# Scores of chunk 0 one projection sooner, copied from PSUM into the tile they are searched in, and its experts chosen in one go

## The chip, the cores and the metric

The kernel runs on one NeuronCore of one Trainium2 chip. The time is that of the whole kernel on the device, in microseconds (us). TensorE is PE, VectorE is DVE, ScalarE is ACT, GpSimd is POOL and SyncE is SP; each takes its instructions in the order in which they are written, and waits on semaphores.

## What is computed

One layer of a decoder trunk on 1024 tokens of 1024 channels. A mixer of four branches ends in an output projection and a layer norm. Then each token picks 16 experts for each of 8 heads out of 16384 (a product of two lists of 128 keys), and adds their value rows, weighted.

```
def peer_ffn(x, w_q, sub_k1, sub_k2, u_tab, v_tab):
    q = (xt @ w_q).reshape(T, PEER_HEADS, 2, PEER_DQ // 2)
    s1 = jnp.einsum('thc,nc->thn', q[:, :, 0], sub_k1, preferred_element_type=jnp.float32)
    s2 = jnp.einsum('thc,nc->thn', q[:, :, 1], sub_k2, preferred_element_type=jnp.float32)
    v1, i1 = lax.top_k(s1, PEER_TOPK)
    v2, i2 = lax.top_k(s2, PEER_TOPK)
    ...
    top_s, top_j = lax.top_k(cand_s, PEER_TOPK)
    idx = jnp.take_along_axis(cand_i, top_j, axis=-1)
    g = jax.nn.softmax(top_s, axis=-1).astype(x.dtype)
    ...
        act = jax.nn.gelu(jnp.einsum('cd,ced->ce', xb, u_tab[ib]), approximate=False)
        return jnp.einsum('ce,ced->cd', gb * act, v_tab[ib])
```

`x = layer_norm(ALPHA * x + mix)` stands ahead of it, and `x = layer_norm(ALPHA * x + ffn)` behind it.

## The kernel before

The 1024 tokens are eight chunks of 128. The first 1305 us are the mixer's branches, which the change leaves alone. The function `ffn` does the rest. It has one program per engine, and the order of all work in it is written out by hand.

First PE folds the query weights and the keys into one matrix (`fold`), so that scores are x times that matrix. Then comes the stage that the change touches, which I call the projections. It has 16 steps, in the order of the list `SEQ`. A step ("m", c) is chunk c's output projection (`mixed`, 48 matmuls at line 1196) and its layer norm on DVE (`first_norm`, lines 1459 to 1462 and 1433 to 1450). A step ("x", c) is chunk c's scores (`scored`, 4 quarters of 48 matmuls, lines 65 to 67), which ACT copies out of PSUM, 512 columns at a time, at line 1322. I write m0, x0 and so on.

Each step needs its input turned round. PE transposes it (`turn`, line 1172, 8 transposes), ACT writes its high half (`high`, line 1296), DVE its low half (`low`, line 1454). There are two buffers, so the turn of a step is issued one step ahead: in step i PE does `turn(i + 1)` and then the matmuls of step i. `turn(i + 1)` waits until `low(i)` is done (semaphore `t_lo`), and where step i + 1 is an x step it also waits for that chunk's layer norm (`normed`). On DVE step i is `low(i + 1)`, then `first_norm` of an m step, then whatever else is hung on that step.

What is hung there is the choice of experts (`choose`, 136 pieces numbered k: lines 1476 to 1587) and the first gathered rows (`row`, line 1652). For even chunks (0, 2, 4, 6) rows of the tables u and v are gathered by POOL (line 1147) into a ring of five buffers at first, and multiplied on DVE; 128 rows of u and 128 of v per chunk. Odd chunks go through PE instead (table blocks, lines 1239 and 1282). POOL starts when `chosen` says that chunk 0's experts are known.

The scores of every chunk go from PSUM to the tile `score_out` (`stage`), from there to HBM, and from there to the tile `scores_in` (`sco`), in which `choose` searches and which it overwrites. Chunk 0's choice is in two parts: pieces 0 to 69 in the step of x1, pieces 70 to 135 in the step of x2. The exponentials of a choice are made by ACT (`exps`, line 1300), at fixed places of ACT's program: chunk 0's after the copies of x2, chunk 1's after table block 2. Chunk 1's choice is spread over rows 3 to 40 (`CHOICE_AT`); its last pieces, from k = 133 on, stand ahead of row 40 and wait for those exponentials. `D_ROWS` says how many rows are done in which step: 8 rows in each of the steps x3 to x7. The rows behind them follow when all scores are done.

The first lines of PE's loop, which sets the order:

```
        for i, (kind, c) in enumerate(SEQ):
            if i + 1 < len(SEQ):
                turn(i + 1)
            (mixed if kind == "m" else scored)(i, c)
```

Of the kernel before, what the change touches and what calls it, by code (L numbers as in the profile page):

```python
# [7 lines left out]
ACT = mybir.ActivationFunctionType  # L8
# [10 lines left out]
NCH = T // P  # L19
# [19 lines left out]
RWS = 1.0 / WS  # L39
# [681 lines left out]
def merge(nc, ctx, M, A):  # L721
# [91 lines left out]
    def _(dve):  # L813
# [21 lines left out]
                        nc.vector.tensor_tensor(out, out, tmp[c % 2][:], ALU.add)  # L835


SEQ = [("m", 0), ("m", 1), ("m", 2), ("x", 0), ("m", 3), ("x", 1), ("m", 4), ("x", 2), ("m", 5), ("x", 3),
       ("m", 6), ("x", 4), ("m", 7), ("x", 5), ("x", 6), ("x", 7)]
M_STEP = {c: i for i, (kind, c) in enumerate(SEQ) if kind == "m"}  # L840
X_STEP = {c: i for i, (kind, c) in enumerate(SEQ) if kind == "x"}
GS = 4096.0
# [3 lines left out]
NT = 136  # L846
# [114 lines left out]
for _w, _n in enumerate((128, 128 + 46, 128 + 78, 256)):  # L961
    for _q in range(32):
        ONEHOT_AT.setdefault(_n + _q, []).append((_w, _q))
D_ROWS = {X_STEP[3]: (0, 8), X_STEP[4]: (8, 16), X_STEP[5]: (16, 24), X_STEP[6]: (24, 32), X_STEP[7]: (32, 40)}


def ffn(nc, ctx, M, A, out):
    sem = lambda n: ctx.enter_context(nc.semaphore(n))
    Tt, ps, ident = M["T"], M["ps"], M["ident"]
    big, hl, ln, stage, sco = (M[n] for n in "big hl ln stage sco".split())  # L970
# [38 lines left out]
    s_mm, s_out, s_stored, x1_stored = (sem(n) for n in "s_mm s_out s_stored x1_stored".split())  # L1009
    sc_in, sc_free, exp_in, exp_out = (sem(n) for n in "sc_in sc_free exp_in exp_out".split())  # L1010
# [22 lines left out]
    @block.sync  # L1033
    def _(sp):
        for b in range(2):
            sp.dma_start(wqt[b], A["w_qt"][b]).then_inc(wq_in[b], 16)
        sp.dma_start(kt[:, 0, :], A["k1_t"]).then_inc(keys_in, 16)
        sp.dma_start(kt[:, 1, :], A["k2_t"]).then_inc(keys_in, 16)
        for i in range(2):
            sp.dma_start(xin[i], A["x"][P * i:P * i + P]).then_inc(x_in[i], 16)  # L1040
        sp.dma_start(ln[:], A["ln"][:, 0:2]).then_inc(ln_in, 16)
        sp.dma_start(iota[:], A["iota"]).then_inc(ln_in, 16)
        for b in range(2, 2 * H):
            sp.wait_ge(fold_mm, 2 * b - 2)
            sp.dma_start(wqt[b % 2], A["w_qt"][b]).then_inc(wq_in[b % 2], 16)
            if b < KD:
                sp.wait_ge(wo_ready, b - 1)
                sp.dma_start(wof[b % 2], A["w_o"][b]).then_inc(wo_in[b % 2], 16)
        for i, (kind, c) in enumerate(SEQ):
            if kind == "m":  # L1050
                if c + 2 < NCH:
                    sp.wait_ge(summed, c + 1)
                    sp.dma_start(xin[c % 2], A["x"][P * (c + 2):P * (c + 3)]).then_inc(x_in[c % 2], 16)
                if c % 2:
                    sp.wait_ge(normed, c + 1)
                    sp.dma_start(A["x1"][c // 2], x1[c]).then_inc(x1_stored, 16)
            else:
                sp.wait_ge(s_out, 4 * c + 4)
                sp.dma_start(A["scores"][c], stage[:]).then_inc(s_stored, 16)
                if c == 0:  # L1060
                    sp.wait_ge(s_stored, 16)
                    sp.dma_start(sco[:], A["scores"][0]).then_inc(sc_in, 16)
                elif c == 2:
                    sp.wait_ge(sc_free, 1)
                    sp.dma_start(sco[:], A["scores"][1]).then_inc(sc_in, 16)
        sp.wait_ge(x1_stored, 16 * ND)
        sp.wait_ge(s_stored, 16 * NCH)
        def choice_load(k):
            sp.wait_ge(sc_free, k)
            sp.dma_start(sco[:], A["scores"][CHOICES[k]]).then_inc(sc_in, 16)  # L1070

        def weights_store(w):
            sp.wait_ge(w_out, 32 * w + 32)
            for a in range(4):
                sp.dma_start(A["weights"][32 * a:32 * a + 32, :, P * w:P * w + P].rearrange("b e t -> e b t"),
                             wst[:, 32 * a:32 * a + 32, :]).then_inc(w_st, 16)

        choice_load(2)
        choice_load(3)
        choice_load(4)  # L1080
        weights_store(0)
        choice_load(5)
        weights_store(1)
        weights_store(2)
        choice_load(6)
        weights_store(3)

        def weights_load(j):
            if j < NEXP // P:
                sp.dma_start(pr[j % NPR], A["weights"][BLOCK[j]]).then_inc(w_in[j // 4 % (NPR // 4)], 16)  # L1090

        def value_load(h, i):
            if h < 2 * NG:
                s, hf = divmod(h, 2)
                sp.dma_start(vt[i], A["v_blocks"][BLOCK[GB * s + i], :, DT * hf:DT * hf + DT]).then_inc(v_in[i // 2], 16)

        sp.wait_ge(w_st, 64 * ND)
        for j in range(4):
            weights_load(j)
            b = BLOCK[j]  # L1100
            sp.wait_ge(h_st[b % 4], 16 * (b // 4 + 1))
            sp.dma_start(ht[j], A["h"][b]).then_inc(h_first, 16)
            value_load(0, j)
        for j in range(4, GB):
            weights_load(j)
            value_load(0, j)
        for j in range(GB, NPR):
            weights_load(j)
        for i in range(4):
            sp.wait_ge(h_st[i], 16 * (NPRE // 4))  # L1110
        sp.dma_start(ln[:], A["ln"][:, 2:4]).then_inc(ln_in, 16)
        for h in range(2 * NG):
            s, hf = divmod(h, 2)
            for i in range(GB):
                sp.wait_ge(v_mm, GB * h + i + 1)
                value_load(h + 1, i)
                if hf:
                    weights_load(GB * s + i + NPR)
            if h == 26:
                sp.wait_ge(sc_free, NCH)  # L1120
                for d in range(2):
                    sp.dma_start(again[d], A["x1"][d]).then_inc(again_in, 16)
        for d in range(ND):
            sp.wait_ge(dense_done, d + 1)
            c = 2 * d + 1
            sp.dma_start(out[P * c:P * c + P, :], dense[d]).then_inc(stored, 16)
            if d < 2:
                sp.dma_start(again[d], A["x1"][d + 2]).then_inc(again_in, 16)
        sp.wait_ge(stored, 16 * ND)
        sp.wait_ge(sparse_stored, 16 * ND)  # L1130
        sp.wait_ge(again_in, 16 * ND)
# [32 lines left out]
    def _(pe):  # L1164
        def turn(i):
            kind, c = SEQ[i]
            if i:
                pe.wait_ge(t_lo, i)
            if kind == "x":
                pe.wait_ge(normed, c + 1)  # L1170
            for k in range(KD):
                m = pe.transpose(ps[:, k // 4, P * (k % 4):P * (k % 4) + P], x1[c][:, P * k:P * k + P], ident[:])
            m.then_inc(turned, 1)
# [44 lines left out]
        pe.wait_ge(fold_lo, 4 * KD)  # L1218
# [3 lines that stand above are left out]
# [68 lines left out]
    def _(act):  # L1290
# [7 lines left out]
        def exps(k):  # L1298
            act.wait_ge(exp_in, k + 1)
            act.activation(gx[:], gx[:], ACT.Exp).then_inc(exp_out, 1)  # L1300
# [13 lines left out]
        for i, (kind, c) in enumerate(SEQ):  # L1314
            if i + 1 < len(SEQ):
                high(i + 1)
            if kind == "x":
                for q in range(4):
                    act.wait_ge(s_mm, 4 * c + q + 1)
                    if c and q == 0:  # L1320
                        act.wait_ge(s_stored, 16 * c)
                    act.activation(stage[:, 512 * q:512 * q + 512], ps[:, 6 + q % 2, :], ACT.Copy, scale=RWS
                                   ).then_inc(s_out, 1)
            if i == X_STEP[2]:
                exps(0)
        for i in range(NUT):
            act.dma_start(ut[i], A["u_t"][i]).then_inc(u_in[i], 16)
# [98 lines left out]
    def _(dve):  # L1426
# [40 lines left out]
        def choose(c, k):  # L1467

            o = CHOICES.index(c)
            if k == 0:  # L1470
                if o == 7:
                    dve.wait_ge(sc_late, 16)
                else:
                    dve.wait_ge(sc_in, 16 * o + 16)
            if k < 16:
                nc.vector.max(v16[:, k, 0:8], sc[:, k, :])
                if k == 15:
# [206 lines left out]
        for i, (kind, c) in enumerate(SEQ):  # L1684
            if i + 1 < len(SEQ):
                low(i + 1)
            if kind == "m":
                first_norm(c)
            if i == X_STEP[1]:
                for k in range(0, 70):  # L1690
                    choose(0, k)
            if i == X_STEP[2]:
                for k in range(70, NT):
                    choose(0, k)
            for n in range(*D_ROWS.get(i, (0, 0))):
                row(n)
        dve.wait_ge(s_mm, 4 * NCH)
        for n in range(D_ROWS[X_STEP[7]][1], NROW):
            row(n)
# [196 lines left out]
```

## Time and profile before

| | us |
|---|---|
| median of three runs | 4133.27 (4126.22 to 4134.67) |
| the profiled execution | 4116.23 |
| its span in the trace | 4114.4 |
| PE, DVE, ACT, POOL busy | 3472.6, 2654.8, 997.8, 1468.6 |
| the projections (first matmul to last copy of scores) | about 1370 to 1642 |
| table blocks and gathered rows behind them | 1642 to the end |

The profiled execution is 17 us (0.4%) below the median of the runs. Times in the trace are counted from the span's start. In the projections PE is busy without a break but for one; behind them PE, DVE and the DMA engines share the work, and none of them is busy all the time.

### The profile page before, as it was taken

To read this page: it belongs to the slowest core of one execution; us is meant where nothing else is said; L and a number is where in the kernel's file an instruction comes from. 1 tells how busy PE (TensorE), PEld (TensorE's weight loads), DVE (VectorE), ACT (ScalarE), POOL (GpSimd) and SP (SyncE) were. 2 spreads that over 40 slices of the span, in tenths; PEclk is the share of its full clock that TensorE was granted. 3 is DMA by queue.
4 is the path that set the end of the run, shared out by engine and by line. 5 is a ranking of instruction groups with operands and counts; after the bars stand their busy time and mean duration, and the time that the engine had idled before them with its cause. 6 is when DMAs were issued, how large, how long until landed. Compare 5 with 4: busy or idle time off the path is not lost.

```text
span 4114.4 us, 43940 instructions
## 1 busy us (share of the span) xinstructions
PE 3472.6 (84%) x15340; PEld 1928.6 (47%) x15340; DVE 2654.8 (65%) x5144; ACT 997.8 (24%) x2241; POOL 1468.6 (36%) x1155
## 2 busy tenths in 40 slices
PE   8988998899998899993778876969867598888685
PEld 3445675688887544441334342424323243333232
DVE  1993463233223488698975973887788667777777
ACT  3324232322222211115496380000000000000000
POOL 2220000012110012354343243656655656566652
PEclk9998697799999999996889988989989799899887
DMA  3110000111102235887968979989988999999995
GB/s 104 51 41 6 1 1 1 72 47 47 63 32 88 94 118 189 289 323 236 306 223 275 315 251 362 375 289 354 364 311 304 330 370 351 331 351 350 340 344 188
DMA packets 323966, 873.03 MB, mean 212 GB/s; under 512 B 30120, under 2 KB 96168, under 8 KB 319024
## 3 DMA queue, kind: packets, MB, share of 16 engines
q0 software_dynamic: 154256, 560.01, 37.8%
q1 hardware_dynamic: 139552, 222.25, 15.6%
q10 hardware_dynamic: 29952, 88.09, 6.0%
q8 instruction: 121, 1.98, 0.2%
q14 instruction: 85, 0.70, 0.1%
HBM read 801.03 MB, written 69.21 MB: 212 GB/s over the span
## 4 chain that ended last, share of the span: by engine, by line
DMA 24%; DVE 16%; PE 10%; ACT 7%; issue 4%; POOL 4%; SPq 1%; DVEq 1%; ACTq 0%
DMA tiles<-v,expert_ids 10%; DMA tiles<-u,expert_ids 7%; DVE tiles L1652 4%; PE ps L1239 4%; POOL tiles L1147 3%; DVE row_t_pairs L1658 3%; ACT score_out L1355 3%; DMA ring_extra<-u,expert_ids 2%; ACT tiles L1354 2%; PE ps L1196 2%; DMA shared_64k<-h_kept 2%; DVE tiles L1625 1%; PE ps L65 1%; PE ps L66 1%; PE ps L67 1%
## 5 line engine op out<-in xcount | busy, mean ns | idle before, releaser
L1282 PE MATMUL ps<-shared_64k 128*128 128x512 f32 x2048 | 943.9, 624 | 300.3 <-ACT score_out L1416 265.7
L1239 PE MATMUL ps<-tiles 128*128 128x512 f32 x2048 | 925.4, 611 | 3.3 <-DMA tiles<-u_t 3.3
L1147 POOL DMA_INDIRECT tiles<-u,expert_ids x437 | 536.1, 1227 | 751.8 <-DVE hidden_sums L1652 371.3
L1282 PEld LDWEIGHTS ps<-shared_64k 128*128 128x128 f32 x2048 | 408.1, 201 | 835.0 <-issue 549.3
L1147 POOL DMA_INDIRECT tiles<-v,expert_ids x438 | 534.8, 1221 | 520.3 <-DVE row_t_pairs L1658 383.5
L1658 DVE SCALAR_TENSOR_TENSOR row_t_pairs<-tiles,hidden_sums,row_t_pairs 128x1024 f32<-128x1024 f32 x432 | 550.4, 1281 | 186.9 <-DMA tiles<-v,expert_ids 184.0
L1239 PEld LDWEIGHTS ps<-tiles 128*128 128x128 f32 x2048 | 399.7, 197 | 497.4 <-issue 497.4
L1652 DVE CUSTOM_DVE_ANT_0 tiles<-tiles 128x1024 f32<-128x1024 f32 x437 | 530.8, 1220 | 151.8 <-DMA tiles<-u,expert_ids 147.3
L785 POOL TENSOR_TENSOR strip_lo<-strip_f,strip_hi 128x3072 f16<-128x3072 f32 x15 | 90.2, 6014 | 825.5 <-ACT strip_f L758 825.5
L65 PE MATMUL ps<-strip_hi,x_hi_t 128*128 128x256 f16 x1024 | 279.9, 273 | 15.2 <-DVE strip_lo L818 10.5
L66 PE MATMUL ps<-strip_lo,x_hi_t 128*128 128x256 f16 x1024 | 279.9, 273 | 0.0
L67 PE MATMUL ps<-strip_hi,x_lo_t 128*128 128x256 f16 x1024 | 279.9, 273 | 0.0
L1416 ACT ACTIVATE score_out<-ps 128x512 f32<-128x512 f32 x128 | 66.0, 602 | 871.1 <-DVE tiles L1625 681.3
L1257 PE MATMUL ps<-tiles 128*128 128x128 f16 x512 | 72.9, 232 | 181.3 <-ACT score_out L1355 100.1
L1354 ACT ACTIVATE tiles<-score_out,picks_t 128x128 f16<-128x128 f16 x512 | 202.8, 396 | 31.0 <-DVE score_out L1601 31.0
L1355 ACT ACTIVATE score_out<-score_out,picks_t 128x128 f16<-128x128 f16 x512 | 202.4, 395 | 0.0
L832 DVE SCALAR_TENSOR_TENSOR product<-ps,gate 128x256 f32<-128x256 f32 x96 | 40.6, 423 | 238.0 <-PE ps L67 177.1
L306 DVE SCALAR_TENSOR_TENSOR conv_acc<-conv_in,dw_sb,conv_acc x120 | 175.5, 1538 | 0.0
L65 PE MATMUL ps<-x_hi_t,w_hi 128*128 128x512 f16 x400 | 152.4, 381 | 13.2 <-DVE x_lo_t L285 13.2
L199 POOL TENSOR_TENSOR w_lo<-w_f,w_hi 128x1024 f16<-128x1024 f32 x28 | 70.4, 2513 | 255.7 <-ACT w_f L116 255.7
L66 PE MATMUL ps<-x_lo_t,w_hi 128*128 128x512 f16 x400 | 152.2, 380 | 0.0
L67 PE MATMUL ps<-x_hi_t,w_lo 128*128 128x512 f16 x400 | 152.1, 380 | 0.0
(263 smaller groups left out, 5234.0 us busy)
## 6 DMA issues: line engine op xcount, KB each, us to landing
tiles<-u_t ACTq DMA_DIRECT2D x128, 512.0 KB, 6.8
shared_64k<-v SPq DMA_DIRECT2D x256, 256.0 KB, 6.4
weights_kept<-shared_64k SPq DMA_DIRECT2D x16, 2048.0 KB, 25.8
shared_64k<-weights_kept SPq DMA_DIRECT2D x128, 256.0 KB, 8.7
strip_f<-strips SPq DMA_DIRECT2D x15, 1536.0 KB, 6.3
h_kept<-ln_sb ACTq DMA_DIRECT2D x80, 256.0 KB, 5.8
shared_64k<-h_kept POOLq DMA_DIRECT2D x76, 256.0 KB, 6.5
w_f<-w_t SPq DMA_DIRECT2D x30, 512.0 KB, 3.6
```

Source lines behind the costliest of these rows:

```text
L65: pe.matmul(out, a_hi, b_hi, start=first, stop=False)
L66: pe.matmul(out, a_hi, b_lo, start=False, stop=False)
L67: return pe.matmul(out, a_lo, b_hi, start=False, stop=last)
L306: nc.vector.scalar_tensor_tensor(acc, src, w, acc, ALU.mult, ALU.add).then_inc(tap, 1)
L785: nc.gpsimd.tensor_tensor(sl[s][:], sf[s][:], sh[s][:], ALU.subtract).then_inc(ready, 1)
L1147: nc.gpsimd.indirect_dma_start(ring[R_SLOT[n]], None, A["u" if r < NSEL else "v"], bass.IndirectOffsetOnAxis(ap=idx[:, g, e:e + 1], axis=0 ...
L1239: m = pe.matmul(ps[:, bank, :], ut[u % NUT][:, k, :], x1t[:, k, :], start=k == 0, stop=k == KD - 1)
L1282: m = pe.matmul(ps[:, 4 + t, :], pr[j % NPR][:, P * t:P * t + P], vt[i], start=i == 0, stop=i == GB - 1)
L1354: act.activation(ah[:, n % 4, t, :], o1[:, n % 4, t, :], ACT.Copy, scale=pt[:, 3, tok])
L1355: ins = act.activation(o1[:, n % 4, t, :], o1[:, n % 4, t, :], ACT.Copy, scale=pt[:, 2, tok])
L1652: nc.vector.tensor_tensor_reduce(src, src, x1[2 * g], 1.0, 0.0, ALU.mult, ALU.add, hid[:, g % 2, e:e + 1]).then_inc(used, 1)
L1658: nc.vector.scalar_tensor_tensor(acc[e % 2], src, hid[:, g % 2, e:e + 1], acc[e % 2], ALU.mult, ALU.add).then_inc(used, 1)
```

## The change

Four things change. `SEQ` puts each x step one place sooner, so x0 comes ahead of m2. ACT copies chunk 0's scores straight into `scores_in`, with no way through HBM. Chunk 0's choice is done in one piece in the step of x1, and its exponentials are made after x1's copies. The first rows are hung on steps x2 to x7, 8 rows each, which is 48 rows in place of 40.

```diff
-SEQ = [("m", 0), ("m", 1), ("m", 2), ("x", 0), ("m", 3), ("x", 1), ("m", 4), ("x", 2), ("m", 5), ("x", 3),
-       ("m", 6), ("x", 4), ("m", 7), ("x", 5), ("x", 6), ("x", 7)]
+SEQ = [("m", 0), ("m", 1), ("x", 0), ("m", 2), ("x", 1), ("m", 3), ("x", 2), ("m", 4), ("x", 3), ("m", 5),
+       ("x", 4), ("m", 6), ("x", 5), ("m", 7), ("x", 6), ("x", 7)]
...
-D_ROWS = {X_STEP[3]: (0, 8), X_STEP[4]: (8, 16), X_STEP[5]: (16, 24), X_STEP[6]: (24, 32), X_STEP[7]: (32, 40)}
+D_ROWS = {X_STEP[c]: (8 * c - 16, 8 * c - 8) for c in range(2, NCH)}
...
-                sp.wait_ge(s_out, 4 * c + 4)
-                sp.dma_start(A["scores"][c], stage[:]).then_inc(s_stored, 16)
-                if c == 0:
+                if c:
+                    sp.wait_ge(s_out, 4 * c + 4)
+                    sp.dma_start(A["scores"][c], stage[:]).then_inc(s_stored, 16)
+                if c == 1:
+                    sp.wait_ge(sc_free, 1)
                     sp.wait_ge(s_stored, 16)
-                    sp.dma_start(sco[:], A["scores"][0]).then_inc(sc_in, 16)
-                elif c == 2:
-                    sp.wait_ge(sc_free, 1)
                     sp.dma_start(sco[:], A["scores"][1]).then_inc(sc_in, 16)
...
-                    if c and q == 0:
-                        act.wait_ge(s_stored, 16 * c)
-                    act.activation(stage[:, 512 * q:512 * q + 512], ps[:, 6 + q % 2, :], ACT.Copy, scale=RWS
+                    if c >= 2 and q == 0:
+                        act.wait_ge(s_stored, 16 * (c - 1))
+                    act.activation((stage if c else sco)[:, 512 * q:512 * q + 512], ps[:, 6 + q % 2, :], ACT.Copy, scale=RWS
                                    ).then_inc(s_out, 1)
-            if i == X_STEP[2]:
+            if i == X_STEP[1]:
                 exps(0)
...
             if k == 0:
-                if o == 7:
+                if o == 0:
+                    dve.wait_ge(s_out, 4)
+                elif o == 7:
                     dve.wait_ge(sc_late, 16)
                 else:
-                    dve.wait_ge(sc_in, 16 * o + 16)
+                    dve.wait_ge(sc_in, 16 * o)
...
             if i == X_STEP[1]:
-                for k in range(0, 70):
-                    choose(0, k)
-            if i == X_STEP[2]:
-                for k in range(70, NT):
+                for k in range(NT):
                     choose(0, k)
```

The first place is PE's program from the matmuls of m0 on. In the kernel before, line 1172 is a turn and line 1196 a projection; the semaphore behind "waits" is what the instruction waits for.

```order
L1172 MATMUL ps<-ident,tiles 128x128 [waits t_lo]
L1172 MATMUL ps<-ident,tiles 128x128 x7
L1196 MATMUL ps<-tiles,row_t_pairs 128x512 [waits t_lo]
L1196 MATMUL ps<-tiles,row_t_pairs 128x512 x47
L1172 MATMUL ps<-ident,tiles 128x128 [waits normed,t_lo]
L1172 MATMUL ps<-ident,tiles 128x128 x7
L1196 MATMUL ps<-tiles,row_t_pairs 128x512 [waits summed,t_lo]
```

These are the turn for m2, the matmuls of m1, the turn for x0 and the start of m2. In the changed kernel the lines are one lower (1171 and 1195):

```order
L1171 MATMUL ps<-ident,tiles 128x128 [waits normed,t_lo]
L1171 MATMUL ps<-ident,tiles 128x128 x7
L1195 MATMUL ps<-tiles,row_t_pairs 128x512 [waits t_lo]
L1195 MATMUL ps<-tiles,row_t_pairs 128x512 x47
L1171 MATMUL ps<-ident,tiles 128x128 [waits t_lo]
L1171 MATMUL ps<-ident,tiles 128x128 x7
L65 MATMUL ps<-shared_64k,row_t_pairs 128x512 [waits t_lo]
```

The turn for x0, with its wait for chunk 0's norm, now stands between the matmuls of m0 and those of m1; it stood behind m1's.

The second place is DVE's program at the end of the first part of chunk 0's choice, before the change. Line 1492 is piece 69, line 1454 is `low`, lines 1459 and 1462 begin `first_norm`.

```order
L1488 MAX best_keys<-scores_in 128x8 x16
L1492 MAX_INDEX best_key_ids<-best_keys,scores_in 128x8 x6
L1454 TENSOR_TENSOR row_t_pairs<-ps,row_t_pairs 128x1024 [waits t_hi]
L1459 TENSOR_SCALAR tiles<-tiles 128x1024 [waits xc_in0]
L1462 SCALAR_TENSOR_TENSOR tiles<-ps,tiles 128x1024 [waits mix_mm]
```

In the changed kernel that `low` (line 1453) and that norm come behind the whole choice, whose last instructions these are:

```order
L1567 TENSOR_REDUCE key_sums<-scores_in 128x128
L1579 SCALAR_TENSOR_TENSOR expert_ids<-key_sums 128x128
L1581 TENSOR_REDUCE gate_sum<-exponents 128x8 [waits exp_out]
L1584 RECIPROCAL gate_sum<-gate_sum 128x8
L1588 TENSOR_TENSOR gates<-exponents,gate_sum 128x128
L1453 TENSOR_TENSOR row_t_pairs<-ps,row_t_pairs 128x1024 [waits t_hi]
L1458 TENSOR_SCALAR tiles<-tiles 128x1024 [waits xc_in1]
L1461 SCALAR_TENSOR_TENSOR tiles<-ps,tiles 128x1024 [waits mix_mm]
```

Between x1's start and the next `low` DVE had 70 pieces, and has 136 now.

## Rows read from the trace of the kernel before

**Rows 1.** Waits, 1370 to 1642 us: who waited for whom, us, times, longest
```profile
POOL tiles L1147 <- DVE gates L1587: 256.2, 1, 256.2
...
PE ps L1172 <- DVE row_t_pairs L1454: 8.7, 1, 8.7
```

**Rows 2.** PE's timeline: start us, us, line, tiles, count, idle before
```profile
1380.29 1.04 PE L1172 MATMUL ps<-ident,tiles 128*128 128x128 f32 x8
...
1402.75 1.04 PE L1172 MATMUL ps<-ident,tiles 128*128 128x128 f32 x8
...
1424.35 1.04 PE L1172 MATMUL ps<-ident,tiles 128*128 128x128 f32 x8
...
1510.07 1.11 PE L1172 MATMUL ps<-ident,tiles 128*128 128x128 f32 x4 [8.67 <-DVE row_t_pairs L1454]
```

**Rows 3.** ACT's timeline: last copies of x1, x2; turn, first and last of x3; x7
```profile
1457.37 0.60 ACT L1322 ACTIVATE score_out<-ps 128x512 f32<-128x512 f32 x1 [4.58 <-PE ps L67]
...
1490.20 0.60 ACT L1322 ACTIVATE score_out<-ps 128x512 f32<-128x512 f32 x1 [4.58 <-PE ps L67]
...
1512.08 1.02 ACT L1296 ACTIVATE row_t_pairs<-ps 128x1024 f16<-128x1024 f32 x1 [18.74 <-PE ps L1172]
...
1533.62 0.60 ACT L1322 ACTIVATE score_out<-ps 128x512 f32<-128x512 f32 x1 [4.58 <-PE ps L67]
...
1641.58 0.60 ACT L1322 ACTIVATE score_out<-ps 128x512 f32<-128x512 f32 x1 [4.58 <-PE ps L67]
```

**Rows 4.** Stretches: us; busy of PE, PEld, DVE, ACT, POOL; granted clock, DMA share, GB/s
```profile
1502.00:1510.00 8.00, 0.00 (x0) 0.00 (x0) 7.51 (x16) 0.00 (x0) 1.02 (x1) 0.80 0.16 48
1510.00:1512.00 2.00, 1.93 (x9) 1.85 (x10) 1.84 (x3) 0.00 (x0) 1.40 (x3) 0.50 1.01 410
1512.00:1514.00 2.00, 2.00 (x8) 0.68 (x6) 1.83 (x4) 1.02 (x1) 1.62 (x2) 0.61 0.85 293
1514.00:1516.00 2.00, 2.00 (x11) 0.94 (x10) 1.68 (x7) 0.00 (x0) 0.00 (x0) 1.00 0.64 207
```

**Rows 5.** DVE's timeline: norm of chunk 0, and from m3's end to `low` of x3
```profile
1387.03 1.28 DVE L1450 SCALAR_TENSOR_TENSOR tiles<-tiles,rstd,ln_sb 128x1024 f32<-128x1024 f32 x1
...
1435.78 1.23 DVE L1462 SCALAR_TENSOR_TENSOR tiles<-ps,tiles 128x1024 f32<-128x1024 f32 x1 [7.48 <-PE ps L1196]
...
1444.63 3.18 DVE L1476 MAX8 best_keys<-scores_in 128x8 f32<-128x128 f32 x16
...
1461.26 1.21 DVE L1454 TENSOR_TENSOR row_t_pairs<-ps,row_t_pairs 128x1024 f16<-128x1024 f32 x1
...
1477.45 0.08 DVE L1492 MATCH_VALUE_LOAD best_key_ids<-best_keys,scores_in 128x8 f32 x1
...
1489.60 0.29 DVE L1530 TENSOR_TENSOR exponents<-best_sums 128x128 f32<-128x128 f32 x1
...
1508.79 1.22 DVE L1454 TENSOR_TENSOR row_t_pairs<-ps,row_t_pairs 128x1024 f16<-128x1024 f32 x1
```

**Rows 6.** DVE's timeline around rows 8 to 15 and around row 40
```profile
1553.69 0.08 DVE L1484 MATCH_VALUE_LOAD scores_in<-best_keys,scores_in 128x8 f32 x1
...
1572.60 1.22 DVE L1454 TENSOR_TENSOR row_t_pairs<-ps,row_t_pairs 128x1024 f16<-128x1024 f32 x1
...
1577.67 1.22 DVE L1462 SCALAR_TENSOR_TENSOR tiles<-ps,tiles 128x1024 f32<-128x1024 f32 x1 [3.26 <-PE ps L1196]
...
1661.93 0.29 DVE L1576 COPY picks<-key_sums 128x256 f32<-128x256 f32 x1
1675.33 0.29 DVE L1580 TENSOR_REDUCE gate_sum<-exponents 128x8 f32<-128x128 f32 x1 [13.10 <-ACT exponents L1300]
```

**Rows 7.** The chain that ended last, behind the projections: start us, us, what
```profile
1650.17 22.51 PE ps L1239 x48
...
1673.69 1.28 ACT L1300
...
1676.39 1.22 DVE tiles L1652
```

**Rows 8.** POOL's timeline: first gather of chunk 0, and first gather behind row 40
```profile
1508.98 1.09 POOL L1147 DMA_INDIRECT tiles<-u,expert_ids  x1 [256.15 <-DVE gates L1587]
...
1680.18 1.68 POOL L1147 DMA_INDIRECT ring_extra<-u,expert_ids  x1 [27.17 <-DVE hidden_sums L1652]
```

**Rows 9.** SP's queue: load of chunk 0's scores
```profile
1429.04 0.33 SPq L1062 DMA_DIRECT2D scores_in<-scores_kept  x1
```

More of the change, by code:

```diff
@@ L1057, in _ @@
             else:
-                sp.wait_ge(s_out, 4 * c + 4)
-                sp.dma_start(A["scores"][c], stage[:]).then_inc(s_stored, 16)
-                if c == 0:
+                if c:
[3 more added lines that the diff above has]
+                    sp.wait_ge(sc_free, 1)
                     sp.wait_ge(s_stored, 16)
-                    sp.dma_start(sco[:], A["scores"][0]).then_inc(sc_in, 16)
-                elif c == 2:
-                    sp.wait_ge(sc_free, 1)
                     sp.dma_start(sco[:], A["scores"][1]).then_inc(sc_in, 16)
         sp.wait_ge(x1_stored, 16 * ND)
-        sp.wait_ge(s_stored, 16 * NCH)
+        sp.wait_ge(s_stored, 16 * (NCH - 1))
         def choice_load(k):
```

## The prediction

> **What bounds the kernel now.** I read the table of waits of the projections first [rows 1]. PE waited once there, 8.7 us, for DVE's `low` (line 1454), and POOL waited from the start for chunk 0's gates. So the stage lasts as long as PE's matmuls plus that one wait, and DVE is the one who is waited for. Then I read the timelines. On PE, x0 with the turn ahead of it takes from 1402.75 to 1424.35, 21.60 us [rows 2]. On ACT, the last copies of x1 and x2 lie 32.83 us apart (1457.37, 1490.20) [rows 3]; that is an m step and an x step with their turns, so an m step with its turn is 32.83 - 21.60 = 11.23 us. From x2's last copy to x3's (1533.62) it is 43.42 us, which is 10.59 us more than a pair takes. Of these, 8.67 us are the wait [rows 2]. The other 1.92 us are the clock: while PE stood idle from about 1501 its granted clock fell, to a mean of 0.80 over 1502 to 1510; it was 0.50 (1.2 GHz) when PE started again, 0.61 over the next two us, and 1.00 (2.4 GHz) from 1514 on [rows 4].
>
> Then I ask who reads the end of this stage. The chain that ended last goes from the last scores through the first table blocks on PE (up to 1672.7) to ACT's exponentials of chunk 1 (1673.69) and on to DVE's row 40 (1676.39) [rows 7]. DVE had come to the pieces ahead of row 40 at 1661.93 and stood 13.10 us for those exponentials [rows 6]; POOL stood 27.17 us for DVE [rows 8]. So both halves of what follows, the table blocks on PE and the gathered rows on DVE, start from PE's end of the projections. What PE loses or wins there goes through to the end; what DVE or POOL win before row 40 ends in that 13.10 us wait.
>
> **The change, part by part.**
>
> *Work.* The matmuls, copies, norms and pieces are the same in number. One store and one load of 1 MB each (chunk 0's scores) go. That load was issued at 1429.04 [rows 9], and DVE came to chunk 0's first piece at 1444.63, directly behind the norm and a `low` [rows 5], with no wait. So leaving the way through HBM out is worth nothing by itself, and its cover was DVE's own order. The exponentials of chunk 0 move to ACT's place behind x1's copies, and ACT stands there until DVE has done piece 123. That is 16.63 + (1489.60 - 1477.45) = 28.8 us into the choice [rows 5], some 19 us ahead of its end. What is queued behind ACT's wait is the high half of the turn for m4, whose low half DVE writes only behind the whole choice, so ACT's wait costs nothing. On SP the load of chunk 1's scores now waits in step x1 until DVE frees the tile, at the end of the choice. Behind it stand the load of x for chunk 5 and the store of chunk 3's norm, and both wait for chunk 3's norm anyway, which DVE does later still: zero.
>
> *First wait, new.* The turn for x0 now stands between m0 and m1, and waits for chunk 0's norm. Without a wait PE could begin that turn at 1380.29, when m0's matmuls are issued [rows 2]. The norm's last instruction starts at 1387.03 and takes 1.28 us, so it ends at 1388.31 [rows 5]; the release after 8.67 us came 0.06 us behind DVE's end (1508.79 + 1.22 = 1510.01, and PE at 1510.07) [rows 2, 5]. So PE starts at 1388.37: **8.08 us lost**. The norm can't be sooner, as it begins with m0's end. For the other x steps this wait costs nothing: a whole x step of 21.60 us lies between m(c) and the turn for x(c), and the norm takes 8.85 us with the `low` behind it (1435.78 to 1444.63) [rows 5].
>
> *Clock after it.* An idle stretch of 8.67 us cost 1.92 us more. For one of 8.08 us I take the same 1.92 us; the bounds are 0, if the clock doesn't fall in the slightly shorter stretch, and 1.92. The nearest row has it fallen for a good part of the 8 us before the restart (0.80 on the mean), so I stay at the upper end.
>
> The Trainium skill bears on this term (TensorE: Matmul & The Clock Gate, section "Why this matters for your kernels"): it warns of idle gaps between bursts of matmuls, after which the array is back at the lower clock, and elsewhere on that page says that the share that runs cold differs from run to run. By its warning the sum keeps the 1.92 us, by its remark on run-to-run differences it could be somewhat less; the trace of this case has one such gap and agrees with the warning.
>
> *Second wait, moved and longer.* Count from e, the end of the m step ahead of x1. DVE's norm and `low` take 8.85 us, then the choice starts. Its first part took 1461.26 - 1444.63 = 16.63 us and its second 1508.79 - 1477.45 = 31.34 us [rows 5], so the whole takes 47.97 us, and `low` behind it 1.22 + 0.06 us. PE is released at e + 58.1. PE itself does x1 and its turn (21.60) and m3 and its turn (11.23), 32.83 us, and then wants exactly this `low`. It waits **58.1 - 32.8 = 25.3 us**. Before, the cut in two let the `low` in between, and the same wait was 8.67 us. The difference is +16.6 us. The clock falls in either case and is back 4 us after the restart, so the 1.92 us behind this wait were there before and cancel. Bounds: 16.0 (if pieces that touch gain some tenths from standing together) to 18.5 (if the clock needs twice as long after a wait three times as long; no row here shows that).
>
> *Rows 0 to 47.* Chunk 0's experts are known sooner. Scores x0 come at -11.23 + 8.08 + 1.92 = -1.2 us against before, m2's end likewise, and the choice starts 1.2 us sooner (1443.4) and ends 48.0 us later, 1491.4 against 1508.79. So the first gather goes out **17.4 us sooner** than at 1508.98 [rows 8]. But DVE then does the same 40 rows beside the same kind of steps, and stops again ahead of row 40 for the exponentials behind table block 2. Rows 40 to 47, moved into x7's step, can't start before that. Worth: zero. DVE has room beside the steps: `low` at 1572.60 came with 3.26 us of idle behind it before m6 ended [rows 6], and rows 8 to 15 took 18.9 us there (from 1553.69).
>
> **Sum.** 8.08 + 1.92 + 16.6 = 26.6 us later at PE's last scores (1641.58 before [rows 3], 1668.2 after), and the same at the exponentials of chunk 1 and at the end. On the profiled execution: 4116.2 + 26.6 = 4142.8. That one is 17 us below the median of the runs; on the median it is 4133.3 + 26.6 = **4159.9 us**.
>
> **Rivals.**
>
> 1. *The sooner gathers carry the end.* If the end followed the start of chunk 0's gathers and not PE, the kernel would win the 17.4 us: 4115.9. For it: POOL waits 256 us for the gates [rows 1], and the rows are on the chain behind 1676 [rows 7]. Against it: DVE's 13.10 us in front of row 40 [rows 6]. It decides only if row 40 no longer waits for table block 2, and the change leaves that wait in place. The Trainium skill (DMA: Bandwidth & Descriptors, "Rules for kernel authors") advises to issue a DMA early and to wait for it late, which is what this change does for the gathers; by that rule alone the time would come out as in this rival. Chance 4%.
> 2. *PE's delay is swallowed later.* PE stands idle for other reasons behind 1675, and if the rows behind row 40 didn't hang on ACT's place, most of the 26.6 us would vanish there: 4133, up to 4140. Against it: rows 6 and 7, in which DVE, too, starts from PE's end. Chance 6%.
> 3. *No first wait.* If m1's matmuls ran before x0's turn, 10.0 us would go and 16.6 stay: 4149.9. The printed order speaks against it. If the norm were hidden but for some part, the time lies between. Chance 6%.
> 4. *More waits than I count.* Rows stand now beside one more m step each (m6 and m7 come behind rows 16 to 31). With 18.9 us for eight rows and about 3.3 us of room, a slice that takes over 22 us makes PE wait at the next `low`, and each such wait brings the clock's 1.9 us: three of 2 + 1.9 us give some 12 us, 4172. Chance 9%.
>
> **How the numbers follow.** My own forecast has 75%. Runs of one kernel differ by 8 us (4126 to 4135), and the clock's term by 2 us. The range has to take in rival 3 on one side and rival 4 on the other: 4146 to 4172. Faster and unchanged need a mechanism that the rows speak against. A measurement of this kernel can tell about 0.2%, 8 us: slower by more than that 0.90 (forecast, rivals 3 and 4), within it 0.06 (rival 2), faster 0.04 (rival 1).
>
> **What the profile after would show.** PE's table of waits has a turn (line 1171) waiting for the norm (line 1449), about 8 us at 1380 to 1388, and one waiting for `low` (line 1453), about 25 us, ending near 1492.6; the granted clock is 0.5 behind both. The last copy of scores is near 1668. The first gather is near 1491.6. DVE still waits for ACT's exponentials in front of row 40, for more than 13 us, until about 1702. I would be wrong if PE's wait for `low` were under 20 us, if the first wait were missing, or if the last scores came 26 us later and the end did not.

## The result: 1.6% slower, more than forecast, and where the time went

The changed kernel takes 4199.41 us (median of four runs, 4169.05 to 4209.74), against 4129.75 us before: a ratio of 1.0161, with a 95% interval of 1.0124 to 1.0198. The forecast was 4159.9 us. The direction was right and the size was not: 70 us in place of 27, and the time lies above the top of the range that I gave (4172). The profiled execution took 4196.32 us, 80.1 us above that of the kernel before. The page of after begins:

```profile
span 4194.5 us, 43938 instructions
...
PE 3517.3 (84%) x15340; PEld 1959.7 (47%) x15340; DVE 2655.4 (63%) x5144; ACT 998.4 (24%) x2241; POOL 1456.2 (35%) x1155
```

I cut both traces at two events on ACT's timeline: the high half of the turn for m1, with which the projections begin (1370.13 before), and the last copy of scores (1641.58 before) [rows 3]. These are the rows of after that count (start us, us, engine, line, tiles, idle before): the begin, the last copies of x0, x1, x2, x5 and x6, and the last of all.

```profile
1415.66 1.02 ACT L1295 ACTIVATE row_t_pairs<-ps 128x1024 f16<-128x1024 f32 x1 [1.91 <-PE ps L1171]
...
1468.79 0.60 ACT L1321 ACTIVATE scores_in<-ps 128x512 f32<-128x512 f32 x1 [4.58 <-PE ps L67]
...
1501.62 0.60 ACT L1321 ACTIVATE score_out<-ps 128x512 f32<-128x512 f32 x1 [4.58 <-PE ps L67]
...
1562.81 0.60 ACT L1321 ACTIVATE score_out<-ps 128x512 f32<-128x512 f32 x1 [4.58 <-PE ps L67]
...
1661.29 0.60 ACT L1321 ACTIVATE score_out<-ps 128x512 f32<-128x512 f32 x1 [4.58 <-PE ps L67]
...
1703.67 0.60 ACT L1321 ACTIVATE score_out<-ps 128x512 f32<-128x512 f32 x1 [4.58 <-PE ps L67]
...
1724.39 0.60 ACT L1321 ACTIVATE score_out<-ps 128x512 f32<-128x512 f32 x1 [4.58 <-PE ps L67]
```

| stretch | before | after | difference |
|---|---|---|---|
| start of the span to the begin of the projections | 1370.1 | 1415.7 | +45.5 |
| the projections | 271.5 | 308.7 | +37.3 |
| from there to the end | 2472.8 | 2470.1 | -2.7 |

So more than half of the loss lies ahead of everything that the change touches. Inside the projections x1 to x2 takes 61.19 us where a pair takes 32.83, which is 28.4 too many, and x5 to x6 takes 42.38, which is 9.6 too many. x0's last copy is 53.13 us behind the begin; in the kernel before it was at 1424.55 with one m step more between, 43.19 us without that step, so this is 9.9 too many. PE's timeline names the three waits:

```profile
1433.99 1.94 PE L1171 MATMUL ps<-ident,tiles 128*128 128x128 f32 x8 [8.01 <-DVE tiles L1449]
...
1538.67 1.54 PE L1171 MATMUL ps<-ident,tiles 128*128 128x128 f32 x6 [25.85 <-DVE row_t_pairs L1453]
...
1680.46 1.94 PE L1171 MATMUL ps<-ident,tiles 128*128 128x128 f32 x8 [7.97 <-DVE tiles L1449]
```

The first two are the ones forecast (8.08 and 25.3 us). The third was not forecast. The chain of after shows it, in order of time: m7's matmuls, then all of chunk 7's norm on DVE, then the turn for x7.

```profile
1662.13 10.37 PE ps L1195 x48
1672.52 1.23 DVE tiles L1461
...
1679.03 1.29 DVE tiles L1449
1680.46 1.94 PE ps L1171 x8
```

What I had said of the other engines held. The first gather went out at 1537.58, 121.9 us behind the begin, and 138.9 us behind it before (1508.98) [rows 8]: 16.9 us sooner, against 17.4 forecast. And DVE stood ahead of row 40, as forecast, now for 35.8 us in place of 13.1 [rows 6]. From DVE's timeline:

```profile
1717.98 0.29 DVE L1577 COPY picks<-key_sums 128x256 f32<-128x256 f32 x1
...
1754.07 0.28 DVE L1581 TENSOR_REDUCE gate_sum<-exponents 128x8 f32<-128x128 f32 x1 [35.80 <-ACT exponents L1299]
```

It had won its rows and could do nothing with them.

### The profile page after: what moved, and what is told of

Read it like the earlier page. It is cut to its first block, busy times and chain, and to the rows that moved or that the text cites. A ratio compares the mean times of both kernels' runs of the same rounds, so it can differ in the third digit from the quotient of the medians.

```text
span 4194.5 us, 43938 instructions
## 1 busy us (share of the span) xinstructions
PE 3517.3 (84%) x15340; PEld 1959.7 (47%) x15340; DVE 2655.4 (63%) x5144; ACT 998.4 (24%) x2241; POOL 1456.2 (35%) x1155
## 4 chain that ended last, share of the span: by engine, by line
DMA 23%; DVE 19%; PE 9%; ACT 7%; issue 5%; POOL 4%; SPq 1%; DVEq 1%; ACTq 0%
DMA tiles<-v,expert_ids 10%; DMA tiles<-u,expert_ids 6%; DVE tiles L1653 4%; DVE row_t_pairs L1659 4%; DMA ring_extra<-u,expert_ids 3%; POOL tiles L1146 3%; ACT score_out L1354 3%; ACT tiles L1353 2%; PE ps L1238 2%; PE ps L1195 2%; DMA shared_64k<-h_kept 2%; DVE tiles L1626 1%; PE ps L65 1%; PE ps L66 1%; PE ps L67 1%
## 5 line engine op out<-in xcount | busy, mean ns | idle before, releaser
L1146 POOL DMA_INDIRECT ring_extra<-u,expert_ids x75 | 91.6, 1222 | 185.8 <-DVE hidden_sums L1653 168.4
```

The lines of the kernel that those rows point to most:

```text
L1146: nc.gpsimd.indirect_dma_start(ring[R_SLOT[n]], None, A["u" if r < NSEL else "v"], bass.IndirectOffsetOnAxis(ap=idx[:, g, e:e + 1], axis=0 ...
```

## The 45 us ahead of the change

The attention stage runs from about 400 to 800 us and is the same code in both kernels. These are stretches of it in the first profile of after. Columns: us, busy time of PE, PEld, DVE, ACT and POOL, then the granted clock, the DMA share and GB/s.

```profile
450.00:500.00 50.00, 50.00 (x179) 37.30 (x177) 15.42 (x43) 11.44 (x27) 0.00 (x0) 0.50 0.00 1
500.00:550.00 50.00, 50.00 (x164) 33.69 (x163) 19.20 (x60) 10.51 (x29) 0.00 (x0) 0.50 0.00 0
550.00:600.00 50.00, 49.97 (x247) 35.52 (x247) 23.15 (x76) 15.08 (x41) 0.00 (x0) 0.76 0.00 1
```

And the same in the kernel before:

```profile
450.00:500.00 50.00, 49.97 (x205) 35.91 (x204) 17.72 (x55) 12.66 (x32) 0.00 (x0) 0.60 0.00 1
500.00:550.00 50.00, 49.83 (x311) 35.54 (x311) 31.38 (x100) 19.73 (x55) 0.00 (x0) 1.00 0.00 1
```

PE is busy in both. But at the lower level of its clock (0.50, 1.2 GHz) it does 164 matmuls in 50 us, at the higher 311. In after the clock came back at 574 us, in before near 490. By an estimate, these 84 us at half the rate cost 42 us, which is nearly all of the 45.5. The question was whether the changed program brings this about. I ran both kernels again.

**The changed kernel again** (twice, no edit).

> The changed kernel as it is, looked at once more, for the part of the 70 us that I did not forecast. In the first look 45.5 us were lost ahead of the projections, in code that the change leaves alone: TensorE's granted clock stayed at 0.50 until about 572 us there, and until 490 us in the kernel before. Theory A (chance): the moment at which the clock comes back in the attention stage differs from run to run in either kernel; then the projections begin anywhere between 1370 and 1416 us in this look, its last scores come 308.7 us (plus or minus 2) behind that begin, and 2470 us (plus or minus 5) from there to the end. Theory B (built in): the changed program always gets its clock back late; then the projections begin at 1416 us again, and all its runs are some 70 us above the kernel before.

> The changed kernel as it is, for the size of its loss and for how often the clock of the attention stage comes back late. Theory A (chance, 37 to 39 us from the projections as the only lasting loss): most runs at 4160 to 4172, a minority 40 to 50 us above that, and the projections begin anywhere from 1367 us; from their begin to the last scores 310 us plus or minus 2. Theory B (built in): most runs near 4200.

**The kernel before again** (no edit).

> The kernel before as it is, looked at once more. Theory A (chance): the clock of the attention stage may come back late here too, so that the begin of the projections differs from 1370 us in some look, and from there to the last scores it is 271.5 us again. Theory B (built in): the clock is back at about 490 us, the projections begin at 1370 us.

The changed kernel again took 4162.82 us (median of four; ratio 1.0097, 1.0071 to 1.0124). Its trace begins the projections at 1367.3, with the clock back by 500 us:

```profile
450.00:500.00 50.00, 49.97 (x205) 35.94 (x203) 17.05 (x51) 12.19 (x30) 0.00 (x0) 0.59 0.00 1
500.00:550.00 50.00, 49.83 (x310) 35.75 (x310) 31.66 (x103) 19.87 (x54) 0.00 (x0) 1.00 0.00 1
```

The third time it took 4185.35 us (six runs; 1.0132, 1.0077 to 1.0187): three runs at 4156 to 4164 and three at 4207 to 4215, and the profiled one, of the latter, begins the projections at 1414.3. The kernel before showed the late clock as well: its profiled execution took 4178.3 us, begins the projections at 1415.8, and reads

```profile
500.00:550.00 50.00, 50.00 (x164) 33.69 (x164) 19.34 (x60) 10.86 (x29) 0.00 (x0) 0.50 0.00 0
550.00:600.00 50.00, 49.97 (x232) 36.25 (x231) 21.59 (x71) 13.86 (x39) 0.00 (x0) 0.70 0.00 1
```

while the median of its eleven runs was 4127.6 (two are far above it: this one, and one of 14951.71 us, for which no trace shows why). So theory A holds: either kernel can lose these 45 us. In the first measurement three of four executions of the changed kernel had lost them, to judge by their times (4196 to 4210, against 4169); only one of the four has a trace. What the change itself costs is about 35 to 40 us: 4162.82 in the second measurement against the 4127.6 of before, a ratio of 1.0097 there, and 37 to 39 us in the stage between the two events. Of all runs, 6 of 14 of the changed kernel and 22 of 93 of the kernel before lie at least 30 us above what is usual for them (about 4162 and 4128). Whether the changed kernel falls into the late clock more often than the other can't be told from so few runs, and stays open; the half of after_third is more than the minority that was expected there.

The stage between the two events is free of the late clock, and varies by some 2 us, mostly with the clock behind its own waits. It was 271.5 and 271.7 us in the two traces of before, and 308.7, 310.9 and 309.1 us in the three of after. The verdicts below go by it.

## Which part of the change makes which wait

**The old order of steps, with the rest of the change.**

```diff
-SEQ = [("m", 0), ("m", 1), ("x", 0), ("m", 2), ("x", 1), ("m", 3), ("x", 2), ("m", 4), ("x", 3), ("m", 5),
-       ("x", 4), ("m", 6), ("x", 5), ("m", 7), ("x", 6), ("x", 7)]
+SEQ = [("m", 0), ("m", 1), ("m", 2), ("x", 0), ("m", 3), ("x", 1), ("m", 4), ("x", 2), ("m", 5), ("x", 3),
+       ("m", 6), ("x", 4), ("m", 7), ("x", 5), ("x", 6), ("x", 7)]
```

> The changed kernel with the list of steps of the kernel before; the direct copy, the choice in one piece and the rows from x2's step on stay. Main theory (two waits for a norm come from the new order, one wait for the low half from the choice in one piece): the waits for a norm behind m0 and behind m7 are gone (10.0 and 9.6 us with their clock), the wait for the low half of about 26 us stays, so from the begin of the projections to the last scores it is 308.7 - 19.6 = 289 us. Rival (the one piece is harmless and the new order makes all three waits): 271.5 us plus nothing. A second rival, that the rows of u are what is late: no change from 308.7.

Measured: 287.8 us for the stage, 4149.86 us for the whole (1.0056, 1.0034 to 1.0078). PE's waits in it (us in total, times, longest) no longer name the norm:

```profile
PE ps L1171 <- DVE row_t_pairs L1453: 25.3, 1, 25.3
PE ps L1171 <- DVE shared_64k L1678: 1.4, 1, 1.4
```

(The second ends the fold, and is in every kernel.) So both waits for a norm come from the order, and the long wait doesn't.

**Only m7 one step sooner.**

```diff
-       ("x", 4), ("m", 6), ("x", 5), ("m", 7), ("x", 6), ("x", 7)]
+       ("x", 4), ("m", 6), ("m", 7), ("x", 5), ("x", 6), ("x", 7)]
```

> The changed kernel with only m7 moved ahead of x5, so that the turn for x7 no longer stands directly behind m7. Main theory: the third wait (8 us for the norm of chunk 7, 9.6 us with its clock) goes and nothing takes its place, 299 us from the begin of the projections to the last scores. Rival: two norms follow each other on VectorE then, with the rows of x4's step ahead of them, and another wait of several us takes its place; 305 us or more.

Measured: 299.2 us, and 4151.15 us for the whole (1.0064, 1.0043 to 1.0085). Of the two waits of 8 us for a norm one is left:

```profile
PE ps L1171 <- DVE row_t_pairs L1453: 25.9, 1, 25.9
PE ps L1171 <- DVE tiles L1449: 8.0, 1, 8.0
```

That is the third wait's cause shown: the turn for x7 stood directly behind m7.

**The choice in two parts again, in the new order.**

```diff
             if i == X_STEP[1]:
-                for k in range(NT):
+                for k in range(0, 70):
+                    choose(0, k)
+            if i == X_STEP[2]:
+                for k in range(70, NT):
                     choose(0, k)
```

The rows, chunk 0's exponentials and chunk 1's load went back to their old places with it.

> The new order and the direct copy stay; the choice of chunk 0 is in two parts again (70 pieces in the step of x1, 66 in that of x2), and rows, exponentials and loads stand where they stood before. Main theory: the wait for the low half is 8.7 us again in place of 25.9 (10.6 in place of 28.4 with the clock behind it), the two waits of 8 us for a norm stay: 308.7 - 17.8 = 291 us from the begin of the projections to the last scores, and the first gather goes out later, not sooner, than in the kernel before. Rival (the sooner x steps alone make the long wait): over 300 us.

Measured: 291.6 us, 4148.3 us for the whole (1.0045, 0.9999 to 1.0091). The long wait is back at its old length, and the norms' two waits stay:

```profile
PE ps L1171 <- DVE tiles L1449: 16.0, 2, 8.0
PE ps L1171 <- DVE row_t_pairs L1453: 8.7, 1, 8.7
```

The first gather went out 137.9 us behind the begin, 1 us sooner than in the kernel before; I had expected it later.

**The direct copy alone, in the kernel before.**

```diff
-                    act.activation(stage[:, 512 * q:512 * q + 512], ps[:, 6 + q % 2, :], ACT.Copy, scale=RWS
+                    act.activation((stage if c else sco)[:, 512 * q:512 * q + 512], ps[:, 6 + q % 2, :], ACT.Copy, scale=RWS
...
```

With it go the store and the load of chunk 0's scores, and the choice waits for ACT's copies in place of the load.

> The kernel before with nothing of the change but the direct copy of chunk 0's scores into the tile in which they are searched. Main theory: VectorE comes to the choice behind a norm and a low half in either case, so that the way through HBM was hidden: 271.5 us from the begin of the projections to the last scores, the choice begins 8.9 us behind m3's end, no difference in the whole. Rival: VectorE reads the scores sooner or ScalarE is held up, 270 us or less, or a difference in the whole of over 4 us.

Measured: 272.3 us, 4128.29 us against 4129.33 (0.9995, 0.9955 to 1.0036). The 0.8 us more in the stage stand behind the one wait, which is 8.67 us as before. The way through HBM was hidden, as the prediction had said.

## What carries the end

**The exponentials of chunk 1 ahead of table block 0, in the kernel before.**

```diff
+        exps(1)
         for u in range(NPRE):
...
-            if u == 2:
-                exps(1)
```

> The kernel before with the exponentials of chunk 1 made ahead of table block 0 in place of behind table block 2. VectorE then does not stand for 13 us ahead of row 40, while TensorE's part is where it was. Theory R (the rows carry the end, TensorE's delay counts only because it holds up these exponentials): 13 us less in the whole, 4114 to 4118. Theory P (TensorE's own matmuls carry the end): no change. Theory RP (both, meeting again later): something between.

**The same edit in the changed kernel.**

> The changed kernel with the exponentials of chunk 1 made ahead of table block 0 in place of behind table block 2. In the changed kernel VectorE stands for 36 us ahead of row 40. Then it would stand only until the last scores are copied, and shortly again for chunk 3's scores: row 44 comes some 24 us sooner. Theory R (the rows carry the end, and the change's sooner gathers are worth something once this wait is gone): 20 to 24 us less than the changed kernel, 4139 to 4143. Theory RP (TensorE's delay of 38 us carries the end as well, beyond some point): 12 us less as in the kernel before, about 4151. Theory P: nothing.

In the kernel before DVE no longer waits in front of row 40:

```profile
1679.20 0.28 DVE L1580 TENSOR_REDUCE gate_sum<-exponents 128x8 f32<-128x128 f32 x1
```

The stage is 271.5 us, and it is 2469.7 us from its last scores to the end. In ten traces with the old place this stretch was 2470 to 2489 us, with the middle at 2482. The whole is 4117.73 us against 4129.33 (median of twelve; the ratio is 0.9978, 0.9948 to 1.0008). Neither settles it alone: the interval takes in 1, and two of the ten traces, the first ones of before (2472.8) and of after (2470.1), are nearly as short.

In the changed kernel DVE's wait is over 6.3 us behind the last scores, in place of 29.7 in the second trace of after, and a short wait for chunk 3's scores follows:

```profile
1683.74 0.29 DVE L1581 TENSOR_REDUCE gate_sum<-exponents 128x8 f32<-128x128 f32 x1 [12.51 <-ACT exponents L1299]
...
1692.11 0.68 DVE L1477 MAX8 best_keys<-scores_in 128x8 f32<-128x128 f32 x3 [2.64 <-DMA scores_in<-scores_kept]
```

The stage still takes 308.9 us, with all three waits of PE in it. But from there to the end it takes 2459.7 us, 10 us less than the shortest of the ten and 22 less than their middle, and the profiled execution took 4138.9 us, 24.9 less than the profiled 4163.8 of after_again, which began its projections 1.3 us sooner. The next best run took 4142.4. The lowest of the fourteen runs of the changed kernel is 4156.1. The other four of its six runs were so far above these (4195.51 to 6541.35, with the median at 4237.95 and a ratio of 1.0104, 1.0041 to 1.0167) that the median says nothing of the edit; I rest this on the traces.

Theory R fits both: against the last scores, rows 13.2 us sooner gave 12 us, and rows 23.4 us sooner gave 22, if the middle of the ten is the measure. A second reading doesn't need that middle. I take the time from DVE's last instruction ahead of row 40 (`picks`, line 1587 or 1588) to the end, in all fourteen traces of this document. It is 2448.6 to 2458.6 us in twelve of them, with the exponentials in either place, while the time from PE's last scores to the end goes from 2459.7 to 2489.0. In the other two, the first traces of before and after, it is 2438.4 and 2439.8; no run shows why these two are shorter. So the rows carry the end. PE's delay reaches it through chunk 1's exponentials: behind table block 2 in the old place, and behind the last copies of scores in the new one, where DVE still waits 12.51 us for them.

**Chunk 0's choice in three parts, in the kernel before, with the direct copy.**

```diff
             if kind == "m":
+                if c == 3:
+                    for k in range(0, 30):
+                        choose(0, k)
                 first_norm(c)
             if i == X_STEP[1]:
-                for k in range(0, 70):
+                for k in range(30, 115):
                     choose(0, k)
             if i == X_STEP[2]:
-                for k in range(70, NT):
+                for k in range(115, NT):
                     choose(0, k)
```

> The kernel before with the direct copy and the choice of chunk 0 in three parts: pieces 0 to 29 ahead of chunk 3's norm, where VectorE stood idle for 7.5 us, 30 to 114 in the step of x1, 115 to 135 in that of x2. Main theory (TensorE's wait is set by how much of the choice stands ahead of a low half): no wait of TensorE in the projections, 271.5 - 10.6 = 261 us from their begin to the last scores, and the whole is 10.6 us less. Rival (a wait comes back at another low half, as one of the margins is only 1.7 us): 265 to 271 us.

Measured: 260.9 us for the stage, and 4116.86 us for the whole (median of twelve; 0.9969, 0.9935 to 1.0003). DVE does 30 pieces while it waits for m3 anyway: m3's sum comes where it came, with 0.56 us of idle in place of 7.48 [rows 5].

```profile
1435.72 1.23 DVE L1461 SCALAR_TENSOR_TENSOR tiles<-ps,tiles 128x1024 f32<-128x1024 f32 x1 [0.56 <-PE ps L1195]
```

Here the direct copy should earn its keep: x0's last copy ended at 1425.15 in the kernel before, and the load by way of HBM, issued at 1429.04 [rows 9], took 4.9 us more to land, so that the scores are in place nearly 9 us sooner, ahead of that gap. I did not run the three parts without the direct copy, so its share is an estimate.

**Both edits together**, run twice.

> The kernel before with both edits that helped: direct copy with chunk 0's choice in three parts (10.6 us of TensorE in the projections), and chunk 1's exponentials ahead of table block 0 (about 12 us of VectorE ahead of row 40). Theory S (the two add up, since one moves TensorE's end of the projections and the other the rows against it): 23 us less than the kernel before, about 4105. Rival (the gain in the rows ends at TensorE's table blocks): 12 us less, 4117.

> The same two edits of the kernel before once more, for the size of their gain, since single runs of either kernel can lose 45 us or more in the attention stage. Theory S (they add up): 261 us plus or minus 1 from the begin of the projections to the last scores, 2470 us plus or minus 6 from there to the end (against about 2481 with the exponentials in their old place), and about 20 us less than the kernel before in the whole. Rival: 12 us less.

The first time 4113.15 us (seven runs; 0.9976, 0.9922 to 1.0029), the second 4107.24 us against 4129.11 (thirteen runs; 0.9948, 0.9912 to 0.9984). The stage was 260.9 us both times, and 2471.6 and 2475.3 us followed it. By the medians the two edits together are worth 18 us the first time, where the interval still takes in 1, and 22 the second, where it doesn't; alone they gave 12.5 and 11.6. So theory S holds in the main, and this version is better than both kernels, by about 0.5%.

## Why the prediction was wrong, step by step

Two steps failed. The sum put nothing down for the time ahead of the projections, on the strength of a spread of 8 us, and this run lost 45.5 us there. And it put nothing down for a wait at x7's turn, which cost 9.6 us. The 27 us that it did count were there.

- *What bounds the kernel, and the way from PE's last scores to the end.* Right. The stretch behind the projections did not change by more than it varies, and DVE waited ahead of row 40 as said. The two runs with the exponentials in a sooner place showed that it is the rows that carry the end, as the chain had suggested [rows 7].
- *First wait.* Right: 8.01 us and 9.9 us with the clock, forecast 8.08 and 10.0. Row 4's clock carried over to a wait that is 0.6 us shorter, as I had chosen.
- *Second wait.* Right in mechanism, a little small: 25.9 us in place of 25.3, and 28.4 us in place of 27.2 with the clock behind it. The difference to before is 17.8 us, forecast 16.6. The clock took 2.5 us there, and 1.9 after 8.7 us in before. Over all traces it takes 1.6 to 3.2 us behind the sixteen waits of 8 or 8.7 us, and 1.7 to 3.1 behind the six of 25 or 26 us. So a gap three times as long doesn't cost clearly more, but my bounds of 0 and 1.92 us were drawn from one gap, and too low at the top.
- *"For the other x steps this wait costs nothing: a whole x step of 21.60 us lies between m(c) and the turn for x(c)."* Wrong, and this is the step that failed by my own doing. It holds for x1 to x6. The list ends in m7, x6, x7, and since a turn is issued one step ahead, the turn for x7 stands between m7 and x6. 9.6 us. I had checked the start of the list row by row and took the rest for periodic. The printed order of PE would have shown a turn that waits for `normed` behind the last projection. Rival 4 priced more waits of this size, but looked for them at DVE's rows, which made PE wait in no trace.
- *"Runs of one kernel differ by 8 us."* Wrong, and the largest part: 45.5 us, from the clock that came back 84 us later in the attention stage. Three runs of before were all I had; eleven and more showed that a run can have 40 to 50 us on top, from a stage that nobody touched. With the projections' loss alone (37.3 us) the forecast from 4129.75 would have been 4167, inside my range, and the second measurement of the same kernel (4162.82) is 3 us from the number that I gave. That is luck: it is 35.0 us above the median of the kernel before in the same measurement (4127.83), 8 us more than my 26.6, and I had started from a median that was 5.5 us higher (4133.3).
- *Rival 1, sooner gathers.* Right in its condition, which the change leaves unmet: with that condition met, the changed kernel's best executions (4138.9 and 4142.4) are still some 10 us above the median of the kernel before. Against the kernel before with the same edit, its trace is 27.4 us longer from the begin of the projections to the end (308.9 + 2459.7 against 271.5 + 2469.7), so the gathers give back about 10 of PE's 37 us.
- *Rivals 2 and 3.* Neither came. PE's delay was not swallowed (the stretch behind the projections took 2470 to 2484 us in the three traces of after, 2473 and 2489 in the two of before), and the first wait is in every trace with the new order.

## What to carry to other kernels

Where input is prepared one step ahead, what counts is not how far a consumer stands behind its producer in the list, but how far the preparation does; walk the list to its last entries, where the pattern breaks. A long job on an engine that others wait for is best cut to the gaps which that engine has anyway, and a transfer that is hidden today may still be worth removing if that makes such a gap usable (here by an estimate, not by a run). And before time is won on a chain, look for the fixed place at which it waits for another one.

## What I had not expected of the hardware

TensorE's clock can stay at its lower level while TensorE is busy. In the second profile of the last version it was 0.50 in every stretch from 450 to 850 us, with TensorE busy 50.00 of 50 us in most of them, and the projections began at 1545.3 us, 179 us later than in the first (1366.3):

```profile
550.00:600.00 50.00, 50.00 (x164) 33.69 (x164) 19.34 (x60) 11.03 (x30) 0.00 (x0) 0.50 0.00 0
600.00:650.00 50.00, 50.00 (x175) 35.69 (x175) 15.55 (x52) 10.70 (x30) 0.00 (x0) 0.50 0.00 0
650.00:700.00 50.00, 50.00 (x163) 34.45 (x162) 17.63 (x47) 10.58 (x26) 0.00 (x0) 0.50 0.00 1
```

Not all of the 179 us are the clock's. About 50 were lost ahead of the attention stage: a POOL instruction (line 199) that takes 2.1 to 4.5 us in the first trace of this version took 69.8 us, and PE stood 62.3 us for it, until 274.6, where it stands 12.4 us in the first trace for DVE's convolution. DVE worked through that convolution (line 306) without a break until 271.8. That this is what held POOL up is not shown, since the same instructions stand side by side in the other traces. The remaining 129 us go with the low clock, which in this trace first came back at about 865 us; less the 50 us that is 815, where the same code had it back at about 490 us in other runs. What decides it is open; I made no experiment on it. Busy time doesn't tell the two apart, but the number of matmuls in a stretch does, and with the granted clock it is the first thing to compare when a difference shows up ahead of a change.
